# A hybrid attention layer on Trainium2: buffers of the first stages at one remainder by 512 bytes, and the down product's operands asked for later, by ScalarE

## The reference

```python
proj = h @ w_in                                   # q, k, v | q, latent, indexer q, k, weights | gates
y_a = swa_sink_attention(qa, ka, va, sinks) @ w_o_a           # window of 128, with sinks
c_kv = rms_norm(cb, kv_norm_g)
k_idx = layer_norm(ki, k_idx_g, k_idx_b)
y_b = dsa_mla_attention(qb, c_kv, qi, k_idx, w_idx, w_uk, w_uv, topk) @ w_o_b   # top 256 keys
mix = (g_a * y_a + g_b * y_b) @ w_out
h = layer_norm(DEEPNORM_ALPHA * h + mix, ln1_g, ln1_b)
ff = (jax.nn.silu(h @ w_ff_gate) * (h @ w_ff_up)) @ w_ff_down # 1024 -> 2816 -> 1024
return layer_norm(DEEPNORM_ALPHA * h + ff, ln2_g, ln2_b)
```

## Time and profile before

| | |
|---|---|
| median of three runs | 3913.82 us |
| the profiled execution | 3914.53 us, span 3912.5 us |
| PE busy | 3542.5 us, 91% of the span |
| DVE, ACT, POOL busy | 2162.0, 1896.9, 1738.3 us (55, 48, 44%) |
| weight loads (PEld, beside PE) | 2941.7 us |
| mean granted TensorE clock | 0.95 |
| moved over DMA | 476.82 MB |
| PE's share of the chain that ended last | 32%; DVE and DMA 4% each |

### The profile page before, as it was taken

How to read it: one execution, slowest core, us unless ns; L and a number is a source line. 1 busy time by engine, 2 the same in 40 slices (tenths; PEclk the granted TensorE clock), 3 DMA queues, 4 the chain that set the end, 5 groups by cost and what they waited for, 6 DMA issues and landing times. The chain is left out here.

```text
span 3912.5 us, 52624 instructions
## 1 busy us (share of the span) xinstructions
PE 3542.5 (91%) x17866; PEld 2941.7 (75%) x17866; DVE 2162.0 (55%) x2890; ACT 1896.9 (48%) x3537; POOL 1738.3 (44%) x2017
## 2 busy tenths in 40 slices
PE   5998788898979999999996897889999999989896
PEld 4876566677768888988995775778887888868685
DVE  4206666887522465666533663475456545545857
ACT  3213577788624698887552222333334333334342
POOL 5213566665311222222003545556665665444544
PEclk9988899899977999999998998999999999989998
DMA  7323322432221111100005656644446443565542
GB/s 237 147 64 108 83 73 71 160 88 78 89 81 33 45 40 32 44 15 19 25 8 183 194 187 206 219 161 169 159 151 196 146 164 114 206 232 186 222 153 92
DMA packets 357530, 476.82 MB, mean 122 GB/s; under 512 B 23704, under 2 KB 246120, under 8 KB 353416
## 3 DMA queue, kind: packets, MB, share of 16 engines
q1 hardware_dynamic: 330864, 430.47, 33.6%
q10 hardware_dynamic: 26400, 43.00, 3.1%
HBM read 319.60 MB, written 153.78 MB: 121 GB/s over the span
## 5 line engine op out<-in xcount | busy, mean ns | idle before, releaser
L2430 POOL TENSOR_TENSOR ff_ring<-ff_raw,ff_ring 128x512 fp32r<-128x512 f32 x264 | 383.6, 1465 | 290.5 <-ACT ff_ring L2549 287.8
L105 PE MATMUL ff_bank<-ff_rounded_pair,ff_ring 128*128 128x512 f32 x1232 | 483.6, 393 | 18.7 <-DVE ff_resid L2709 7.4
L107 PE MATMUL ff_bank<-ff_rounded_pair,ff_ring 128*128 128x512 f32 x1232 | 482.5, 392 | 0.0
L106 PE MATMUL ff_bank<-ff_rounded_pair,ff_ring 128*128 128x512 f32 x1232 | 482.4, 392 | 0.0
L1641 PE MATMUL at_ctx<-at_p_t,at_c_nat 128*128 128x128 f32 (+1 forms) x2432 | 351.9, 286 | 7.9 <-ACT at_ctx_t L1752 7.0
L1641 PEld LDWEIGHTS at_ctx<-at_p_t,at_c_nat 128*128 128x128 f32 (+1 forms) x2432 | 306.6, 194 | 37.7 <-ACT at_ctx_t L1752 13.0
L1746 ACT ACTIVATE at_p_t<-at_turn 128x512 f32<-128x512 f32 (+4 forms) x416 | 212.9, 544 | 206.3 <-PE at_turn L1619 172.6
L2435 POOL TENSOR_TENSOR ff_ring<-ff_raw,ff_ring 128x512 fp32r<-128x512 f32 x154 | 210.8, 1373 | 215.1 <-ACT ff_ring L2599 215.0
L2777 DVE TENSOR_TENSOR ff_rounded_a_ring<-ff_f_q,ff_rounded_a_ring 128x512 fp32r<-128x512 f32 x154 | 200.1, 1306 | 157.9 <-ACT ff_rounded_a_ring L2591 156.9
L105 PEld LDWEIGHTS ff_bank<-ff_rounded_pair,ff_ring 128*128 128x128 f32 x1232 | 233.0, 189 | 70.7 <-issue 13.4
L105 PE MATMUL ff_bank<-ff_ring,ff_rounded_a_ring 128*128 128x512 f32 x616 | 245.1, 398 | 39.1 <-DVE ff_rounded_a_ring L2777 31.5
(11 more groups left out here) (351 smaller groups left out, 9109.7 us busy)
## 6 DMA issues: line engine op xcount, KB each, us to landing
f_kept<-ff_resid SPq DMA_DIRECT2D x154, 256.0 KB, 2.5
ff_f_q<-f_kept SPq DMA_DIRECT2D x14, 2816.0 KB, 9.9
pj_raw<-in_w_in SPq DMA_DIRECT2D x50, 512.0 KB, 4.5
proj<-se_row SPq DMA_DIRECT2D x96, 256.0 KB, 2.3
ff_raw<-in_w_ff_gate SPq DMA_DIRECT2D x22, 1024.0 KB, 10.8
ff_raw<-in_w_ff_up SPq DMA_DIRECT2D x22, 1024.0 KB, 6.2
ff_raw<-down_comb SPq DMA_DIRECT2D x88, 256.0 KB, 2.7
ff_raw<-in_w_ff_down SPq DMA_DIRECT2D x66, 256.0 KB, 3.1
```

The lines of the kernel that those rows point to most:

```text
L105: pe.matmul(out, lhs_lo, rhs_hi, start=start, stop=False, skip_group_check=goes_on)
L106: pe.matmul(out, lhs_hi, rhs_hi, start=False, stop=False, skip_group_check=goes_on)
L107: return pe.matmul(out, lhs_hi, rhs_lo, start=False, stop=stop, skip_group_check=goes_on)
L2430: pool.tensor_tensor(ring[:, step % RING, 1, :].rearrange("p (k c) -> p k c", c=P), f_operand(it, q, m), f32(ring[:, step % RING, 0, :]).r ...
```

## The change

Three parts.

1. **Placement.** The calls of `Scope.sb` in the `pj`, `se` and `at` scopes are put in another order, some small buffers among them, so that others begin elsewhere. Remainders of their starts by 512 bytes, before and after:

| buffers | before | after |
|---|---|---|
| `h_hi`, `h_lo` | 384 | 384 |
| `first_hi/lo`, `w_hi/lo`, `raw`, `row`, all of the `ln` scope | 448 | 384 |
| `ki_hi`, `ki_lo` | 0, 64 | 384 |
| `cin`, `cn`, `ch`, `cl` | 128, 320 | 384 |
| `qi_2` | 384 | 384 |
| `c_hi`, `c_lo` | 384, 448 | 384 |
| `ql_hi/lo`; `qa`, `qb` | 256; 128 | 384 |
| `p_t`, `ctx_t`, `o_nat`, `o_t`; `wuv` | 448; 0 | 384 |
| everything of the `ff` scope | 128 | 128 |

   The constant -0.5 (`half`) is now kept once in each inner scope, with one `memset` more.

   PE's list is the same before and after. The diff, cut:

```diff
@@ -193,7 +193,6 @@
     with Scope(nc, "pj") as s:
         h_hi, h_lo = [s.sb(f"h_hi{u}", [P, KT, GROUP], F32R) for u in range(2)], [s.sb(f"h_lo{u}", [P, KT, GROUP], F32R) for u in range(2)]
         ident = s.sb("ident", [P, P])
-        half = s.sb("half", [P, 16])[:, 0:2]
...
+            half_ln = a.sb("half", [P, 1])
...
         with Scope(nc, "se") as a:
             w_hi, w_lo = [first_hi, a.sb("w_hi", [P, KT, P], F32R)], [first_lo, a.sb("w_lo", [P, KT, P], F32R)]
             row = [a.sb(f"row{v}", [P, GROUP]) for v in range(3)]
-            bias, bias_rows = a.sb("bias", [P, SPLIT_CHUNKS]), a.sb("bias_rows", [SPLIT_CHUNKS, P])
-            ki_hi, ki_lo = a.sb("ki_hi", [P, L], F32R), a.sb("ki_lo", [P, L], F32R)
-            cg, kg, kb = a.sb("cg", [P, P]), a.sb("kg", [P, DH]), a.sb("kb", [P, DH])
+            bias_rows = a.sb("bias_rows", [SPLIT_CHUNKS, P])
+            ki_hi = a.sb("ki_hi", [P, L], F32R)
+            kg, bias, stats, mean_var = a.sb("kg", [P, DH]), a.sb("bias", [P, SPLIT_CHUNKS]), a.sb("stats", [P, 6]), a.sb("mv", [P, 2])
+            square, var_eps = a.sb("square", [P, 1]), a.sb("ve", [P, 2])
+            ki_lo = a.sb("ki_lo", [P, L], F32R)
+            kb, rstd, neg_scale, undo = a.sb("kb", [P, DH]), a.sb("rstd", [P, 2]), a.sb("neg_scale", [P, HEADS // 2]), a.sb("undo", [P, 2])
+            count, wanted, sign = a.sb("count", [P, 2]), a.sb("wanted", [P, 2]), a.sb("sign", [P, 2])
+            cg = a.sb("cg", [P, P])
             cin, kin, vin = a.sb("cin", [P, P]), a.sb("kin", [DH, P]), a.sb("vin", [P, P])
-            stats, mean_var, square = a.sb("stats", [P, 6]), a.sb("mv", [P, 2]), a.sb("square", [P, 1])
-            var_eps, rstd = a.sb("ve", [P, 2]), a.sb("rstd", [P, 10])[:, 0:2]
             cn, kn, vn = [a.sb(f"cn{u}", [P, P]) for u in range(2)], [a.sb(f"kn{u}", [P, 2, DH]) for u in range(2)], a.sb("vn", [P, P])
             ch, cl = [a.sb(f"ch{u}", [P, P], F32R) for u in range(2)], [a.sb(f"cl{u}", [P, P], F32R) for u in range(2)]
-            query_key = a.sb("query_key", [P, L])
             qi = a.sb("qi", [P, HEADS, P])
             qi_2 = [a.sb(f"qi_2{u}", [P, HEADS, P], F32R) for u in range(2)]
             w_idx = a.sb("w_idx", [P, TILES, HEADS])
...
+            half = a.sb("half", [P, 2])
...
+                    pool.memset(half[:, :], -0.5)
...
-        c_nat, c_hi, c_lo = s.sb("c_nat", [P, 17 * P]), s.sb("c_hi", [P, L], F32R), s.sb("c_lo", [P, L], F32R)
+        c_nat = s.sb("c_nat", [P, 17 * P])
         wuv = s.sb("wuv", [P, HEADS, DH])
+        qa, qb = s.sb("qa", [P, HEADS // 2, P]), s.sb("qb", [P, HEADS // 2, P])
+        v_win = s.sb("v_win", [WH, 2, P])
+        ql_hi, ql_lo = [s.sb(f"ql_hi{u}", [P, HEADS, P], F32R) for u in range(2)], [s.sb(f"ql_lo{u}", [P, HEADS, P], F32R) for u in range(2)]
+        p_t = [s.sb(f"p_t{u}", [P, 4, P]) for u in range(PT)]
+        ctx_t = s.sb("ctx_t", [P, HEADS, P])
+        o_nat = [s.sb(f"o_nat{b}", [P, HEADS * DH]) for b in range(2)]
+        o_t = [s.sb(f"o_t{b}", [P, 4, P]) for b in range(2)]
+        c_hi = s.sb("c_hi", [P, L], F32R)
...
+        c_lo = s.sb("c_lo", [P, L], F32R)
+        u_b = [s.sb(f"u_b{u}", [P, L]) for u in range(3)]
+        min_b = s.sb("min_b", [P, 2 * HEADS, 3])
+        k_win = s.sb("k_win", [P, 2, WA])
...
@@ -2319,11 +2321,11 @@
                         if g == NG - 1 and c == 1:
                             load_raw(0)
                             load_raw(1)
-                        if g == NG - 1 and c == 3:
-                            load_h(0)
-                            load_h(1)
-                for piece in range(2, 6):
-                    load_h(piece)
+                        if g == NG - 1 and c in (3, 6):
+                            load_h(2 * c // 3 - 2)
+                            load_h(2 * c // 3 - 1)
+                load_h(4)
+                load_h(5)
                 load_raw(2)
...
@@ -2355,17 +2357,16 @@
                     if r == 11 and 2 * it + 4 < 2 * NPASS * NI:
                         load_raw(2 * it + 4)
                     if it == NPASS * NI - 1:
-                        if r in (5, 7, 12, 13):
-                            n = (5, 7, 12, 13).index(r)
+                        if r in (5, 7):
+                            n = r // 2 - 2
                             if n == 0:
                                 features_kept(NI)
-                            sp.wait_ge(product_ready, f_step(it, (1, 2, 4, 5)[n], 1) + 1 + START)
+                            sp.wait_ge(product_ready, f_step(it, 1 + n, 1) + 1 + START)
                             load_product(n)
                         if r == 8:
                             for d in range(RING):
                                 load_b(d)
                 sp.wait_ge(product_ready, F_STEPS + START)
-                load_product(SLOTS - 1)
 
                 for d in range(D_STEPS):
                     p, q, k = of_step(d)
@@ -2379,9 +2380,8 @@
                         features_kept(NPASS * NI)
                         sp.wait_ge(nat_stored, 16 * NG + START)
                         load_resid(0, 0)
+                    if n == 1 and k == 2:
                         load_resid(0, 1)
-                    if k == 4 and SLOTS <= n + 4 < NPASS * NQ:
-                        load_product(n + 4)
                     if p == 1 and q == 0 and k == 4:
                         sp.wait_ge(out_stored[0], 16 * TPG + START)
                         load_resid(1, 0)
@@ -2447,7 +2447,10 @@
                             low_part(c % 2, use1(g, KT + c + 2))
                         if g == 2 and c % 2:
                             combine(c // 2)
-                for step in range(LEAD):
+                        if g == NG - 1 and c == 4:
+                            low_weight(0)
+                            low_weight(1)
+                for step in range(2, LEAD):
                     low_weight(step)
                 for step in range(F_STEPS):
                     it, r = divmod(step, PER_IT)
@@ -2597,6 +2600,16 @@
                     else:
                         act.wait_ge(d_used, d - RING + 1 + START)
                     act.activation(ring[:, d % RING, 0, :], b_raw[:, d % RING, :], ACT.Copy).then_inc(b_hi_ready, 1)
+
+                def load_late_product(n):
+                    if n >= SLOTS:
+                        act.wait_ge(a_lo_ready, (n - SLOTS + 1) * NI + START)
+                    its = NI * (1 if n < NQ else NPASS)
+                    for c in range(3):
+                        act.wait_ge(feat_stored[c], 16 * its + START)
+                    for j in range(4):
+                        act.wait_ge(fsum_stored[j], 16 * its + START)
+                    act.dma_start(f_q[n % SLOTS][:, :, :], f_kept[n // NQ, n % NQ]).then_inc(fq_loaded[n % SLOTS], 16)
 
                 def store_out(p, h, a):
                     act.wait_ge(h2_ready, TPG * (2 * p + h) + a + 1 + START)
@@ -2632,9 +2645,9 @@
                         if g == NG - 1 and c in (4, 5):
                             high_h(2 * c - 6)
                             high_h(2 * c - 5)
-                        if g == NG - 1 and c >= 6:
-                            high_weight(2 * c - 12)
-                            high_weight(2 * c - 11)
+                        if g == NG - 1 and c in (3, 7):
+                            high_weight(c // 2 - 1 if c == 3 else 2)
+                            high_weight(1 if c == 3 else 3)
                 for step in range(F_STEPS + 2):
                     it, r = divmod(step, PER_IT)
                     p, i = divmod(it, NI)
@@ -2672,6 +2685,8 @@
                     if d + LEAD < D_STEPS:
                         high_b(d + LEAD)
                         high_a(d + LEAD)
+                    if k == 8 and NQ * p + q + 2 < NPASS * NQ:
+                        load_late_product(NQ * p + q + 2)
                     if q == NQ - 1 and k - 2 in NORM_AT:
                         store_out(p, 0, NORM_AT.index(k - 2))
                     if p and q == 0 and k - 2 in NORM_AT:
@@ -2820,10 +2835,12 @@
                         mix(g + 1, a)
                     for n in range(TPG, KT):
                         mix(g + 1, n)
-                for piece in range(6):
-                    low_h(piece)
+                low_h(0)
+                low_h(1)
                 weight_sums(0, 0)
                 weight_sums(0, 1)
+                for piece in range(2, 6):
+                    low_h(piece)
                 add1(NG - 1)
                 for step in range(F_STEPS + 2):
                     it, r = divmod(step, PER_IT)
```

33 lines of the change are left out of this document (10 added, 23 removed).

## The result

The changed kernel takes 3883.24 us by the median of four runs (3880.22 to 3885.49), against 3913.84 for the kernel before: a ratio of 0.9918, 95% interval 0.9901 to 0.9936, so 0.8% faster. The forecast was 3868 us with a range of 3853 to 3893: the sign and the range held, the gain was 31 us where 45 were forecast. The narrower range given for the forecast case alone, 3855 to 3880, did not hold it. The profiled execution after took 3880.22 us, span 3878.3.

The account below looks back on a forecast made before the run. TensorE was taken as the bound, by its distance of matmul starts and its standing at the seams around SwiGLU. Terms -18 - 4 - 22 - 1 = -45 us; 3914.5 - 45 - 0.7 was given as 3868 us, range 3853 to 3893.

Parts of the forecast that it names:

- Placement, forecast -18: Projection stages and attention: operands placed at other remainders shorten the distance of matmul starts, -18 us, bounds 0 and -26.
- the 6 ns: Full-clock distance of 128x512 matmul starts: 233 ns in the first stage against 227 in SwiGLU, 6.6 by longer stretches.
- the rival of 3887 us: Projection stages and attention: placement does nothing, the gap has another cause, only -4 - 22 - 1 remain; chance 0.27.
- I keep two thirds: 9 us: Second projection stage: of 2304 x 6.6 ns = 15.2 us, less 12% for half clock, two thirds survive the relu waits.
- The row of the relu: Second projection stage: TensorE's wait for ScalarE's indexer relu (`se_rel`), 94.6 us before, was to grow by some 5 us.
- The 65 waits of 128 steps: Second projection stage: 65 of 128 indexer steps end waiting for ScalarE's relu, so between half and all the gain survives.
- Attention was forecast at -3: Attention: 552 full-width logit matmuls x 6.6 ns = 3.6 us, narrower ones nearly as much, at under half the gap.
- The indexer's 1 us: Second projection stage: the indexer's own matmuls were to gain 1 us from placement.
- Seam, forecast -4: Mixing to SwiGLU: weight sums ahead of four low parts bring `add1` 1.5 to 3 us earlier; -4 us, bounds -0.5 and -6.
- Start of the down product, forecast -22: Down product, start: 19.3 us of waits and 3.9 us of clock go, 1 us left; -22 us, bounds -15 and -24.
- Rest of the down product, forecast -1: Down product after its start: operand and residual loads no longer meet in one queue; -1 us, bounds +4 and -3.
- The slower rival: Down product: operand loads on ScalarE's queue arrive late, TensorE stands once per product; 3928 us at 35 us a load; chance 0.04.

Follow-up runs that it names:

- e1: The kernel before with only the placement part of the change; 3906.66 us against 3913.39, ratio 0.9985.
- e4: The changed kernel with VectorE taking the low parts of pieces 0 to 3 ahead of the weight sums, only 4 and 5 behind; 3880.65 us, ratio 0.9913.
- e9: e4 with both residual loads put back into step 3 of the down product; 3890.76 us, ratio 0.9943.
- e3: The kernel before with only the part at the seam from mixing to SwiGLU; 3911.05 us, ratio 0.9994.

## Why the prediction was right in range and wrong in size

**Placement, forecast -18, measured about -6** (e1: -5.9 by its ratio, -2 to -9). This is 12 of the 15 us by which the forecast was off. *That* placement is the reason for the 6 ns was right, and the rival of 3887 us, that it does nothing, fell in the first stage: 5.1 us were forecast there and 5.4 to 6.2 came. The time alone would not have told: 3883 lies nearer to that rival's 3887 than to the forecast's 3868, and the stated range held it because it had been widened for the rivals. The rule of the Trainium skill behind that rival ("SBUF — State Buffer", section "Who interferes with whom": TensorE never waits on anyone) would make this term 0; the first stage's 227 or 233 ns by placement alone do not agree with that. Whether it is a wait of one of TensorE's reads for the other no run shows.

The failed step is "I keep two thirds: 9 us" for the second stage, in both of its factors. The gain per matmul there is 3.7 ns and not 6.6, as the runs of matmuls are short; 2304 of them would give 8.5 us at full clock, 7.5 with the 12% taken off, and the work fell by less still, 5.1 us at full clock; where the rest went stays open. And the waits take most of that: TensorE's time outside gaps falls from 752.0 us (mean of three traces) to 747.3 (mean of seven, 742.5 to 753.0), its gaps grow by 3.8. What remains is about 1 us, and with a stage that scatters by 4 us it may be nothing: it is -1.6 by the mean of the seven and -0.7 by that of the three with the old placement (0, -1.6, -0.4). The row of the relu did not show it as the prediction said: it grew by 0.8 us in the changed kernel, not by some 5. The 65 waits of 128 steps were read as half of the steps keeping their gain; that the others are tied to the same ScalarE chain by their order, and so keep next to nothing, would explain it, but no run tests it. Attention was forecast at -3; its work at full clock did not change. The indexer's 1 us did not come either: its full-width matmuls took 232.1 ns by the mean at full clock where they had taken 230.9.

**Seam, forecast -4, measured 0.** The failed step is the sentence that no piece is asked for later than before. Pieces 4 and 5 are, by 6.4 us, since their buffers come free with the low parts that were moved behind the sums. The chain was written down without the wait of `load_h` in it. e4 and the eight kernels built on it show the gain that was there for another order, 4.3 us by the mean.

**Start of the down product, forecast -22, measured -22.1.** Right by every step: both waits gone, the clock at 1.00, one new wait of 1.35 us where 1 was put. e9's trace prices the residual's share at 7 us. (The prediction looked for this place 40 us earlier, at 3370; its own -18 and -4 give 22 earlier. It came 10.7 earlier, at 3403.3.)

**Rest of the down product, forecast -1, measured -1.3**; it is -1.0 to -1.2 in e1 and e3, too, where nothing was changed there, so it is no effect of the change but of where the trace before lay. The slower rival needed a load of 32 us; the median was 11.1.

**The sums.** 3914.5 - 45 - 0.7 is 3869, not 3868. The lower end of 3853 does not follow either: with -26 for placement and the boundary at -6 the sum is 3913.8 - 26 - 6 - 22 - 1 = 3859, and 3855 is what all four lower bounds give in full, not in their middle two thirds. The measured 3883 lies on the other side, so nothing hangs on these.

## What to carry to other kernels

When a load is asked for long before it is needed, look at what stands behind it in its queue: three operands of which the first was needed only some 50 us later (19 steps of 2.72 us), and two residual loads together, cost 22 us, and asking later (by whichever engine) gave them back. Before an instruction is moved behind others, follow the buffer it frees to the load that waits for that buffer, and see whether that load then becomes the last. A gain per matmul was worth its full sum where nothing else paced the stage and the work came in long runs; where ScalarE's chain was met every few microseconds, all but about 1 us of it went. And before a difference of a few microseconds between two traces is given to a change, compare how long each stood at half clock: in attention that alone made 6 us between two of these traces (63 against 76 us at 0.50).

## What was not expected of the hardware

The distance of fp32r matmuls of 512 columns depends on where their operands begin in SBUF. With the moving operand at 384, in long runs, it is 226.7 ns with the weights level or 256 away, 233.3 at 64, 232.3 at 128, 229 at 192; the four classes by 256 were seen at eight differences, one of them foretold. It is not the difference alone, as the indexer's 233.7 ns with both at 0 shows, nor the weights alone, as its 236.7 and 230.8 for the same matmuls with the weights at 384 show; the full rule was not found. In the projections it takes about eight matmuls after other work until the level placement gives its 227. What settles in those was not found.
